# Attention scores issued two steps ahead in some branches, and a later wait at the start of the down products

## The chip, the cores and the metric

The kernel runs on one core of a Trainium2 chip. The time is that of the device in microseconds (us) for one launch of the whole program. Engines are named as in the profile: PE (TensorE matmul), PEld (its weight loads), DVE (VectorE), ACT (ScalarE), POOL (GpSimd), SP (the queue that issues the DMAs).

## The reference

Two layers of a transformer block on 256 latent tokens and 256 context tokens, 1024 wide, all in float32. A layer is a gated feed-forward (up and gate to 2816, down to 1024), a token mixer, and a second feed-forward; each has an RMS norm before and after it, with shift, scale and gate from a conditioning vector. The mixer has four attention branches side by side. Cut to what matters here:

```
A: softmax(q1 k1) - lam * softmax(q2 k2), times v, then a norm      (differential)
B: softmax over a grid window with a bias, plus all context keys   (neighbourhood)
C: grouped queries, q and k normalised per head                    (GQA)
D: band of +-128 tokens plus context keys plus one sink logit       (sliding window)
y = sum_i sigmoid(u @ gate_i) * (branch_i @ w_branch_i);   out = y @ w_out
```

In layer 0 the context tokens pass through the mixer too (512 query columns, T = 512); in layer 1, the last, only the 256 latent tokens are queries (T = 256).

## The kernel before, in words

**Weights.** All weights come in units of 128 x 1024 floats at most (`fetch`, SP), four slots deep. ACT copies a unit to `w_high` in fp32r (L290), DVE writes the rest to `w_low` (L296), both two units ahead of PE (`AHEAD`). One product is then three matmuls for each 128 x 128 block: high x high (L307), low x high (L308), and, in a second pass, high x low (L316). `used` counts finished units.

**The feed-forward.** `Hidden` makes 22 tiles of the hidden vector; DVE finishes a tile with three operations (L693, L697, L699) and then raises `ready`. `Down` reads them: each output row is four units (`DOWN_K` = 6, 5, 6, 5 tiles), so that parts 0 to 2 read tiles 0 to 16 and part 3 reads tiles 17 to 21. Its `tensor` begins with one wait (L787) for all 22 tiles.

**A branch (`Branch`).** The PE program of a branch has two halves. First the *carriers*: the four `mix` units of the branch before (its output times `w_branch`, `mix_unit`, banks 6 and 7 for even c, 4 and 5 for odd c), and then `ahead` gate units of this branch (`window_part`), beside which DVE and ACT prepare q and k (`ropes`, `keep_qk`). Each gate unit is taken out of its bank by ACT (`window_taken`: tanh at L1154, a plain copy at L1156 for the projections of the next branch). On ACT the order for carrier g is: split of a later unit, `window_taken(g)`, then the `keep_qk` items of g. `ahead` is 5, 6 and 2 for B, C and D in layer 1, and 2 for D in layer 0. Gate 0 is taken only when the branch before is wholly merged, since `gate` is reused.

Then the *steps*: J = 16 in layer 0, 8 in layer 1. One step is two heads of 128 queries against 512 (or 256) keys:

- PE `scores(j)` (L1084) into banks 0 and 1, after `expd(j)`, that is when the exponentials of step j-1 have read those banks;
- DVE `row_max(j)`: bias in B (L1380) or mask in D (L1386), the maximum (L1390), and one small operation (L1401), in D three (L1395, L1398, L1399);
- ACT `exps(j)`: two exponentials (L1230) into `prob`, in D a small one before (L1228);
- DVE `scale_probs(j)`: reciprocal and two multiplications (L1422, L1425), in D an addition before (L1409);
- PE `flip(j)`: transposes (L1094) into banks 2 and 3; ACT `keep_probs(j)` (L1240) copies them out;
- every second step PE `mix(p)` (L1107) into bank 4 + p % 2; ACT `high_of_out` (L1253) and DVE `low_of_out` (L1432) read it.

Between them stand the rest of the window units, spread over the steps by a fixed table of weights (`points`), each in two parts, "high" (L307, L308) and "low" (L316), in bank 6 + w % 2. For the later unit w the wait is for `taken(w - 1)`, so that one product can run while the one before it is taken out. Each engine executes its list in order:

```
PE : scores(j+1), part, [mix], flip(j), part
DVE: row_max(j+1), split, scale_probs(j+1), [low_of_out], split
ACT: exps(j+1), part's results, keep_probs(j), [high_of_out], part's results
```

After the last branch `Merge` runs the four mix units of D and `Out` the output product.

Of the kernel before, what the change touches and what calls it, by code (L numbers as in the profile page):

```python
# [158 lines left out]
def build(nc, tokens, small, cond, weights, mods, na_rows, h_kept, c_kept, out, stop=None):  # L159
    STARTS, N_UNITS = unit_starts()  # L160
    WIDTHS = [DOWN_K[u % 4] if name.startswith("down") else 8 for layer in range(DEPTH) for name, count in layer_units(layer) for u in range(count)]
    with ExitStack() as ctx:
# [611 lines left out]
        class Down(Result):  # L774
# [11 lines left out]
            def tensor(self, pe):  # L786
                pe.wait_ge(self.hidden.ready.sem, self.hidden.ready.at(FT))  # L787

                def two_rows(i, last):
                    for e, unit in enumerate(self.units):  # L790
                        n0 = self.n0 + e
                        n = n0 + len(self.units) * i
                        r, part = unit
                        if part == 0 and past(2 * i + r - 1):
                            pe.wait_ge(self.freed.sem, self.freed.at(2 * i + r - 1))
                        k0 = sum(DOWN_K[:part])
                        product(pe, n, n0, [(ps[:, r, 0:self.T], [(w, k0 + w) for w in range(DOWN_K[part])])],
                                lambda k: hid_high[:, k, 0:self.T], lambda k: hid_low[:, k, 0:self.T],
                                first=part == 0, last=part == 3)
                self.rows(two_rows)  # L800
# [70 lines left out]
        class Branch(Stage):  # L871
# [4 lines left out]
            def __init__(self, layer, index, T, norm, before):  # L876
# [3 lines left out]
                self.tiles = BT + 2 * self.nk  # L880

                self.roped, self.normed = b != "B", b == "C"

# [60 lines left out]
                self.sunk = signals.new("sink_shifted", J if b == "D" else 0)  # L944
                self.expd = signals.new("exp_ready", J)
                self.sums = signals.new("sum_steps", 3 * J)
                self.probs = signals.new("probs_ready", J)
# [40 lines left out]
            def values(self, v, tt):  # L988

                return v[:, tt, 0:self.nk * P], ps[:, tt, 0:self.nk * P]  # L990

            def head_items(self, c):

                return [i for i in range(len(self.prep)) if self.normed and i // 2 == c]
# [21 lines left out]
            def window_part(self, pe, w, part):  # L1016
                kind, t, W = self.window[w]
                n = self.n_window + w
                outs = [(ps[:, 6 + w % 2, 0:W], [(k, k) for k in range(KT)])]
                if part == "low":  # L1020
                    product_low(pe, n, n, outs, lambda k: u_high[:, k, 0:W])
                    return
                if w >= 2:
                    pe.wait_ge(self.taken.sem, self.taken.at(w - 1))
                elif self.before:
                    pe.wait_ge(self.before.merged.sem, self.before.merged.at(6))
                else:
                    pe.wait_ge(self.projected.sem, self.projected.at(self.tiles))
                product_high(pe, n, n, outs, lambda k: u_high[:, k, 0:W], lambda k: u_low[:, k, 0:W])
# [5 lines left out]
            def mix_unit(self, pe, c):  # L1035

                if c == 0:
                    pe.wait_ge(self.taken.sem, self.taken.at(len(self.window)))
                if c >= 2:
                    pe.wait_ge(self.merged.sem, self.merged.at(2 * c - 2))  # L1040
                T, n, b0 = self.T, self.n_mix + c, 6 - 2 * (c % 2)
                product(pe, n, n, [(ps[:, b0 + r, 0:T], [(4 * r + k, k) for k in range(BT)]) for r in range(2)],
                        lambda k: q_high[:, k, 0:T], lambda k: q_low[:, k, 0:T])

            def tensor(self, pe):
# [31 lines left out]
                def scores(j):  # L1077
                    t, q, key, nkeys = self.steps[j]
                    kt = t if self.nk == BT else 0
                    if past(j):  # L1080
                        pe.wait_ge(self.expd.sem, self.expd.at(j))
                    for s in range(2):
                        rows = slice(s * HD, (s + 1) * HD)
                        m = pe.matmul(ps[:, s, 0:nkeys], q_all[rows, t, q:q + P], k_all[rows, kt, key:key + nkeys], start=True, stop=True)  # L1084
                    m.then_inc(self.scored.sem, 1)
# [11 lines left out]
                def mix(p):  # L1097
                    t, _, key, nkeys = self.steps[2 * p]
                    vt = t if self.nk == BT else 0
                    pe.wait_ge(self.pt_made.sem, self.pt_made.at(2 * p + 2))  # L1100
                    if p >= 2:
                        pe.wait_ge(self.o_done.sem, self.o_done.at(p - 1))
                    n, ns = nkeys // P, 1 if b == "A" else 2
                    for c in range(n):
                        for s in range(ns):
                            rows = slice(s * P // ns, (s + 1) * P // ns)
                            m = pe.matmul(ps[rows, 4 + p % 2, 0:S_X], v_all[:, key // P + c, vt * P:(vt + 1) * P][:, rows], pt[:, p % 2, s, c],  # L1107
                                          start=c == 0, stop=c == n - 1)
                    m.then_inc(self.mixed.sem, 1)
# [7 lines left out]

                scores(0)
                self.window_parts(pe, 0)
                for j in range(J):  # L1120
                    if j + 1 < J:
                        scores(j + 1)
                    self.window_parts(pe, 1 + 2 * j)
                    if b == "A" and j % 2 and j >= 3:
                        sub_sum((j - 3) // 2)
                    if j % 2 == 0 and j:
                        mix(j // 2 - 1)
                    flip(j)
                    self.window_parts(pe, 2 + 2 * j)
# [19 lines left out]
            def window_taken(self, act, w):  # L1149
# [3 lines left out]
                if kind == "gate":  # L1153
                    i = act.activation(gate[:, t, 0:W], ps[:, 6 + w % 2, 0:W], ACT.Tanh, scale=0.5)  # L1154
                else:
                    i = act.activation(proj[:, t, 0:W], ps[:, 6 + w % 2, 0:W], ACT.Copy)  # L1156
                i.then_inc(self.taken.sem, 1)
# [29 lines left out]
            def scalar(self, act):  # L1187
# [33 lines left out]
                def exps(j):  # L1221
# [7 lines left out]
                    for s in range(2):  # L1229
                        e = act.activation(prob[:, j % 2, s, 0:nkeys], ps[:, s, 0:nkeys], ACT.Exp,  # L1230
                                           bias=stat[:, j % 2, 1, s:s + 1], scale=SCALE, accum_out=stat[:, j % 2, 2, s:s + 1])
# [11 lines left out]
                def high_of_out(p):  # L1243
# [3 lines left out]
                    if b == "A":  # L1247
# [4 lines left out]
                        return  # L1252
                    act.activation(q_high[:, t, q:q + S_X], ps[:, bank, 0:S_X], ACT.Copy).then_inc(self.o_high.sem, 1)  # L1253

# [76 lines left out]
            def merge(self, dve, c):  # L1331

                b0, T = 6 - 2 * (c % 2), self.T
                dve.wait_ge(used.sem, self.n_mix + c + 1)
# [14 lines left out]
            def vector(self, dve):  # L1349
# [22 lines left out]
                def row_max(j):  # L1372
                    t, q, key, nkeys = self.steps[j]
                    f = sum(step[2] == 0 for step in self.steps[:j])
                    both = ps[:, 0:2]
                    dve.wait_ge(self.scored.sem, self.scored.at(j + 1))
# [15 lines left out]
                    if b == "D":  # L1392
                        sink = smv("sink", self.l, DEPTH, "p (t s) -> p t s", s=2)[:, t]

                        dve.scalar_tensor_tensor(out=stat[:, j % 2, 5], in0=stat[:, j % 2, 0], scalar=SCALE, in1=sink,  # L1395
                                                 op0=ALU.mult, op1=ALU.max).then_inc(self.sums.sem, 1)
                        dve.wait_ge(self.sums.sem, self.sums.at(3 * j + 1))
                        dve.tensor_tensor(stat[:, j % 2, 3], sink, stat[:, j % 2, 5], ALU.subtract).then_inc(self.sunk.sem, 1)  # L1398
# [4 lines left out]
                def scale_probs(j):  # L1403
# [4 lines left out]
                    if b == "D":  # L1408
                        dve.tensor_tensor(st[:, 5], st[:, 2], st[:, 4], ALU.add).then_inc(self.sums.sem, 1)  # L1409
                        dve.wait_ge(self.sums.sem, self.sums.at(3 * j + 2))  # L1410
# [17 lines left out]
                def low_of_out(p):  # L1428
                    t, q, _, _ = self.steps[2 * p]
                    bank = 4 + p % 2  # L1430
                    dve.wait_ge(self.o_high.sem, self.o_high.at(p + 1))
                    dve.tensor_tensor(q_low[:, t, q:q + S_X], ps[:, bank, 0:S_X], q_high[:, t, q:q + S_X], ALU.subtract)\  # L1432
                        .then_inc(self.o_low.sem, 1)
# [12 lines left out]

                row_max(0)
                self.window_splits(dve, split_low, 0)
                scale_probs(0)
                for j in range(J):  # L1450
                    if j + 1 < J:
                        row_max(j + 1)
                    self.window_splits(dve, split_low, 1 + 2 * j)
# [114 lines left out]
        for layer in range(DEPTH):  # L1568
            last = layer == DEPTH - 1
            for j in range(3):  # L1570
# [3 lines left out]
                if j == 1:  # L1574
                    T = S_X if last else S_ALL
                    branches = []
                    for i in range(len(BRANCHES)):
                        branches.append(Branch(layer, i, T, norm, branches[-1] if branches else None))
                        mixers[layer, BRANCHES[i]] = branches[-1]
                    stages += branches  # L1580
                    merge = Merge(layer, T, branches[-1])
# [221 lines left out]
```

## Time and profile before

| | |
|---|---|
| median of 3 runs | 2626.4 us (2624.17 to 2632.94) |
| the profiled execution | 2630.91 us, of which span 2629.1 us |
| PE busy | 2458.7 us (94%) |
| DVE busy | 1584.3 us (60%) |
| ACT busy | 1068.2 us (41%) |
| mean granted clock of PE | 0.975 |

The span is from the first to the last instruction. A granted clock of 1.00 is 2.4 GHz, 0.50 is 1.2 GHz; a stretch between them had both. "Idle before" an instruction is time in which its engine ran nothing, and the name behind it is what released it.

### The profile page before, as it was taken

The page shows a single profiled execution, that of the slowest core. Times are in us where ns is not written, and L with a number is a line of the kernel's source. Part 1 is how long each engine was busy: PE and PEld are TensorE (multiplying, and loading weights), DVE is VectorE, ACT ScalarE, POOL GpSimd, SP SyncE. Part 2 cuts the span into 40 slices and gives each one's busy share as a digit, 9 for nine tenths or more (in the row PEclk, how much of TensorE's full clock was granted, in tenths as well). Part 3 has the DMA queues.
Part 4 walks back from the last instruction along what each step waited for, and adds up shares of the span by engine and source line. Part 5 has one row for each costly group of instructions (what it writes and reads, how often), then busy time and mean ns, then how long its engine had stood idle before and what let it go on. Part 6 is the DMA issues. An engine that isn't in the chain of part 4 may idle for free.

```text
span 2629.1 us, 31723 instructions
## 1 busy us (share of the span) xinstructions
PE 2458.7 (94%) x12584; PEld 1987.2 (76%) x12584; DVE 1584.3 (60%) x2620; ACT 1068.2 (41%) x1842; POOL 27.3 (1%) x43
## 2 busy tenths in 40 slices
PE   6999998999999998889999989999989999978998
PEld 3788786877767675667887868887868777767998
DVE  2888777345455455689886873333455456567654
ACT  4222234355354534452222352222345555545444
POOL 0000000000000000000000000000000000000000
PEclk8999999999999999999999999999999999989999
DMA  5655454221212121126555522222333243223554
GB/s 225 224 192 192 165 189 141 90 72 65 99 62 72 56 81 64 60 93 216 192 192 170 185 93 96 97 96 84 101 113 128 74 147 109 89 97 112 178 171 157
DMA packets 98069, 331.42 MB, mean 126 GB/s; under 512 B 11009, under 2 KB 12033, under 8 KB 97281
## 3 DMA queue, kind: packets, MB, share of 16 engines
q1 hardware_dynamic: 97922, 329.39, 36.3%
q8 instruction: 100, 1.64, 0.2%
q14 instruction: 47, 0.39, 0.0%
HBM read 323.06 MB, written 6.29 MB: 125 GB/s over the span
## 4 chain that ended last, share of the span: by engine, by line
PE 78%; DVE 10%; ACT 7%; issue 3%; DMA 2%; SPq 0%; POOL 0%; DVEq 0%; ACTq 0%
PE ps L307 23%; PE ps L316 23%; PE ps L308 23%; PE ps L1107 2%; PE ps L1084 2%; DVE stat L1390 2%; ACT prob L1230 2%; PE ps L1094 2%; PE ps L620 2%; ACT w_high L290 1%; DVE w_low L296 1%; DMA raw<-in_weights 1%; DVE tmp L602 1%; ACT pt L1240 1%; ACT sq L551 1%
## 5 line engine op out<-in xcount | busy, mean ns | idle before, releaser
L296 DVE TENSOR_TENSOR w_low<-raw,w_high 128x1024 fp32r<-128x1024 f32 (+1 forms) x488 | 552.4, 1135 | 598.2 <-ACT w_high L290 597.6
L307 PE MATMUL ps<-u_high,w_high 128*128 128x512 f32 (+1 forms) x2304 | 816.6, 365 | 13.1 <-DVE hid_low L699 11.1
L290 ACT ACTIVATE w_high<-raw 128x1024 fp32r<-128x1024 f32 (+1 forms) x488 | 482.0, 990 | 816.5 <-DMA raw<-in_weights 815.9
L308 PE MATMUL ps<-u_low,w_high 128*128 128x512 f32 (+1 forms) x2304 | 807.6, 361 | 0.0
L316 PE MATMUL ps<-u_high,w_low 128*128 128x512 f32 (+1 forms) x2496 | 545.0, 362 | 4.8 <-DVE w_low L296 4.8
L307 PEld LDWEIGHTS ps<-u_high,w_high 128*128 128x128 f32 x2304 | 444.3, 193 | 104.0 <-issue 22.1
L316 PEld LDWEIGHTS ps<-u_high,w_low 128*128 128x128 f32 x2496 | 422.8, 190 | 93.2 <-issue 20.1
L308 PEld LDWEIGHTS ps<-u_low,w_high 128*128 128x128 f32 x2304 | 444.4, 193 | 62.2
L379 DVE CUSTOM_DVE_ANT_0 ps<-mod_raw,c_all,smalls 128x1024 f32<-128x1024 f32 x256 | 319.0, 1287 | 1.1 <-DMA mod_raw<-in_mods 1.0
L307 PE MATMUL ps<-hid_high,w_high 128*128 128x512 f32 (+1 forms) x704 | 252.3, 367 | 9.0 <-DVE hid_low L699 9.0
L308 PE MATMUL ps<-hid_low,w_high 128*128 128x512 f32 (+1 forms) x704 | 251.9, 367 | 0.0
L1230 ACT ACTIVATE prob<-ps,stat 128x512 f32<-128x512 f32 (+1 forms) x192 | 116.3, 610 | 161.8 <-DVE stat L1401 161.8
L316 PE MATMUL ps<-hid_high,w_low 128*128 128x512 f32 (+1 forms) x704 | 161.6, 363 | 0.0
L307 PEld LDWEIGHTS ps<-hid_high,w_high 128*128 128x128 f32 x704 | 134.6, 191 | 31.6 <-DVE hid_low L699 10.4
L308 PEld LDWEIGHTS ps<-hid_low,w_high 128*128 128x128 f32 x704 | 134.6, 191 | 21.1
L1084 PE MATMUL ps<-k_all,q_all 64*128 64x512 f32 (+1 forms) x384 | 96.2, 578 | 45.1 <-ACT prob L1230 33.3
L316 PEld LDWEIGHTS ps<-hid_high,w_low 128*128 128x128 f32 x704 | 122.5, 189 | 20.7
L1390 DVE TENSOR_REDUCE stat<-ps 128x2 f32<-128x1024 f32 (+1 forms) x96 | 100.2, 1044 | 38.8 <-PE ps L1084 37.4
L693 DVE TENSOR_TENSOR hid<-silu_g,ps 128x512 f32<-128x512 f32 (+1 forms) x88 | 54.2, 616 | 91.8 <-PE ps L316 91.4
L1240 ACT ACTIVATE pt<-ps 128x1024 f32<-128x1024 f32 (+2 forms) x96 | 76.3, 795 | 73.7 <-PE ps L1094 73.5
L620 PE MATMUL ps<-u_high,w_high 128*128 128x512 f32 (+1 forms) x192 | 56.8, 423 | 37.6 <-ACT u_high L555 37.6
L1094 PE MATMUL ps<-smalls,prob 128*128 128x128 f32 x560 | 80.5, 279 | 10.5 <-DVE prob L1425 9.1
(147 smaller groups left out, 2160.1 us busy)
## 6 DMA issues: line engine op xcount, KB each, us to landing
raw<-in_weights SPq DMA_DIRECT2D x360, 512.0 KB, 3.5
mod_raw<-in_mods SPq DMA_DIRECT2D x128, 512.0 KB, 4.5
raw<-in_weights SPq DMA_DIRECT2D x64, 384.0 KB, 3.0
raw<-in_weights SPq DMA_DIRECT2D x64, 320.0 KB, 2.8
mod_first<-in_mods SPq DMA_DIRECT2D x16, 512.0 KB, 13.4
h_kept<-h SPq DMA_DIRECT2D x16, 256.0 KB, 2.0
na_bias<-in_na_rows SPq DMA_DIRECT2D x16, 256.0 KB, 4.0
h<-h_kept SPq DMA_DIRECT2D x2, 2048.0 KB, 8.2
```

Source lines behind the costliest of these rows:

```text
L290: act.activation(w_high[:, s, 0:width], raw[s][:, 0:width], ACT.Copy).then_inc(high_made.sem, 1)
L296: dve.tensor_tensor(w_low[s][:, 0:width], raw[s][:, 0:width], w_high[:, s, 0:width], ALU.subtract).then_inc(low_made.sem, 1)
L307: pe.matmul(o, w_high[:, s, w], x_high(x), start=first and a == 0, stop=False)
L308: pe.matmul(o, w_high[:, s, w], x_low(x), start=False, stop=False)
L316: done = pe.matmul(o, w_low[s][:, w], x_high(x), start=False, stop=last and a == len(terms) - 1)
L379: done = dve.tensor_tensor_reduce(out=ps[:, 4 + 2 * s:6 + 2 * s].rearrange("p a b -> p (a b)"), in0=mod_raw[i % MOD_SLOTS][:, :], in1=c_al ...
L620: pe.matmul(ps[:, banks[e], 0:W], w_high[:, (self.n0 + e) % SLOTS, k], x[:, k, 0:W], start=k == 0 and x is u_high, stop=False)
L1084: m = pe.matmul(ps[:, s, 0:nkeys], q_all[rows, t, q:q + P], k_all[rows, kt, key:key + nkeys], start=True, stop=True)
L1094: m = pe.transpose(ps[:, 2 + s, c * P:(c + 1) * P], prob[:, j % 2, s, c * P:(c + 1) * P], ident)
L1230: e = act.activation(prob[:, j % 2, s, 0:nkeys], ps[:, s, 0:nkeys], ACT.Exp, bias=stat[:, j % 2, 1, s:s + 1], scale=SCALE, accum_out=stat[ ...
L1240: act.activation(pt[:, j // 2 % 2, 0:ns, 0:nkeys // P, half], ps[:, 2:2 + ns, 0:nkeys].rearrange("p s (c q) -> p s c q", q=P), ACT.Copy).t ...
L1390: dve.tensor_reduce(stat[:, j % 2, 0], both[:, :, 0:nkeys], AX.X, ALU.max).then_inc(self.maxed.sem, 1)
```

## The change

In D of both layers and in B and C of layer 1 (`deep`) the scores go two steps ahead, in banks 0 and 1 for even steps and 6 and 7 for odd steps. For that the window units have one bank (5) in place of two, `mix` has one bank (4) in place of two, and the mix units of the branch before change places (even c in 4 and 5, odd c in 6 and 7). DVE's row maxima go two steps ahead as well. In D the semaphore `sum_steps` is split in two, as the order of its increments changes. In `Down` the wait for all 22 hidden tiles becomes a wait for 21 tiles ahead of parts 0 to 2 of the first row, and for 22 ahead of its part 3.

```diff
             def tensor(self, pe):            # Down
-                pe.wait_ge(self.hidden.ready.sem, self.hidden.ready.at(FT))
...
+                        if i == 0 and r == 0:
+                            pe.wait_ge(self.hidden.ready.sem, self.hidden.ready.at(FT if part == 3 else FT - 1))
...
+                self.deep = b == "D" or b in "BC" and T == S_X
+                self.early = 2 if self.deep else 1
...
+            def score_bank(self, j):
+                return 6 * (j % 2) if self.deep else 0
+            def window_bank(self, w):
+                return 5 if self.deep else 6 + w % 2
+            def out_of(self, p):
+                return ps[:, 4 if self.deep else 4 + p % 2, 0:S_X]
+            def mix_bank(self, c):
+                return 4 + 2 * (c % 2) if self.mix_swapped else 6 - 2 * (c % 2)
...
             def window_part(self, pe, w, part):
-                if w >= 2:
-                    pe.wait_ge(self.taken.sem, self.taken.at(w - 1))
+                banks = 1 if self.deep else 2
+                if w >= banks:
+                    pe.wait_ge(self.taken.sem, self.taken.at(w - banks + 1))
...
             def scores(j):
-                    if past(j):
-                        pe.wait_ge(self.expd.sem, self.expd.at(j))
+                    if past(j + 1 - self.early):
+                        pe.wait_ge(self.expd.sem, self.expd.at(j + 1 - self.early))
...
             def mix(p):
-                    if p >= 2:
-                        pe.wait_ge(self.o_done.sem, self.o_done.at(p - 1))
+                    if p >= (1 if self.deep else 2):
+                        pe.wait_ge(self.o_done.sem, self.o_done.at(p if self.deep else p - 1))
...
-                scores(0)
+                for j in range(self.early):
+                    scores(j)
                 self.window_parts(pe, 0)
                 for j in range(J):
-                    if j + 1 < J:
-                        scores(j + 1)
+                    if j + self.early < J:
+                        scores(j + self.early)
...
-                row_max(0)
+                for j in range(self.early):
+                    row_max(j)
                 self.window_splits(dve, split_low, 0)
                 scale_probs(0)
                 for j in range(J):
-                    if j + 1 < J:
-                        row_max(j + 1)
+                    if j + self.early < J:
+                        row_max(j + self.early)
...
+                    for i, branch in enumerate(branches):
+                        branch.mix_swapped = i + 1 < len(branches) and branches[i + 1].deep
```

The lists of the other engines keep their order, so that ACT still does `exps(j+1)` ahead of `keep_probs(j)`. Which parts of the window stand between the steps stays as it was.

## Rows read from the trace of the kernel before

**Rows 1.** The page: busy times, and the down products' first matmuls with their waits.
```profile
PE 2458.7 (94%) x12584; PEld 1987.2 (76%) x12584; DVE 1584.3 (60%) x2620; ACT 1068.2 (41%) x1842; POOL 27.3 (1%) x43
...
L307 PE MATMUL ps<-hid_high,w_high 128*128 128x512 f32 (+1 forms) x704 | 252.3, 367 | 9.0 <-DVE hid_low L699 9.0
```

**Rows 2.** Windows over the steps of D (layer 0), then B, C, D (layer 1).
```profile
core 0: us, PE busy (x) PEld busy (x) DVE busy (x) ACT busy (x) POOL busy (x), PEclk, DMA share, GB/s
...
984.00:1081.00 97.00, 78.33 (x401) 50.77 (x402) 51.33 (x150) 44.79 (x118) 0.00 (x0) 0.95 0.15 54
...
2125.00:2190.00 65.00, 57.75 (x376) 44.28 (x376) 37.19 (x62) 32.02 (x64) 0.00 (x0) 0.97 0.26 90
...
2228.00:2287.00 59.00, 54.38 (x356) 40.38 (x357) 29.84 (x52) 30.74 (x60) 0.00 (x0) 1.00 0.21 73
...
2308.60:2368.60 60.00, 48.37 (x304) 35.73 (x304) 35.91 (x84) 28.55 (x65) 0.00 (x0) 0.89 0.23 86
```

**Rows 3.** Waits, 984 to 1081 us, D of layer 0: total us, times, longest.
```profile
PE ps L1084 <- ACT prob L1230: 10.5, 7, 3.2
...
PE ps L1094 <- DVE prob L1425: 4.4, 4, 2.3
```

**Rows 4.** Waits, 2125 to 2190 us, B of layer 1.
```profile
PE ps L1084 <- ACT prob L1230: 4.2, 5, 0.9
...
PE ps L1094 <- DVE prob L1425: 2.1, 1, 2.1
```

**Rows 5.** Waits, 2228 to 2287 us, C of layer 1.
```profile
PE ps L1084 <- ACT prob L1230: 3.0, 3, 1.0
```

**Rows 6.** Waits, 2308.6 to 2368.6 us, D of layer 1.
```profile
PE ps L1084 <- ACT prob L1230: 8.2, 4, 3.5
...
PE ps L1094 <- DVE prob L1425: 1.8, 2, 1.3
```

**Rows 7.** Window after the first down start, L307 alone: us, PE, PEld, PEclk, DMA.
```profile
297.70:302.00 4.30, 3.32 (x6) 1.69 (x6) 0.60 0.28 107
```

**Rows 8.** Timeline of DVE in D, layer 0: start, us, operation, [idle before].
```profile
985.40 0.43 DVE L1386 TENSOR_TENSOR ps<-ps,smalls 128x256 f32<-128x256 f32 x1 [4.40 <-PE ps L1084]
985.87 1.23 DVE L1390 TENSOR_REDUCE stat<-ps 128x2 f32<-128x1024 f32 x1
...
991.65 0.88 DVE L1425 TENSOR_SCALAR prob<-prob,stat 128x512 f32<-128x512 f32 x2
```

**Rows 9.** Timeline of PE around three hand-overs of a bank, same columns.
```profile
984.22 1.13 PE L1084 MATMUL ps<-k_all,q_all 64*128 64x512 f32 x4 [1.72 <-ACT q_all L1185]
...
2118.02 1.12 PE L316 MATMUL ps<-u_high,w_low 128*128 128x256 f32 x8
...
2362.82 1.10 PE L1094 MATMUL ps<-smalls,prob 128*128 128x128 f32 x8 [1.32 <-DVE prob L1425]
2365.03 1.95 PE L1107 MATMUL ps<-pt,v_all 128*64 128x256 f32 x16 [1.11 <-ACT pt L1240]
```

**Rows 10.** Timeline of ACT in the carriers of D, B, C, D.
```profile
982.54 0.60 ACT L1154 ACTIVATE gate<-ps 128x512 f32<-128x512 f32 x1 [2.79 <-PE ps L316]
...
2113.46 1.28 ACT L1154 ACT_TABLE_LOAD   x1 [0.89 <-PE ps L316]
2114.76 0.39 ACT L1154 ACTIVATE gate<-ps 128x256 f32<-128x256 f32 x1
...
2119.18 0.38 ACT L1154 ACTIVATE gate<-ps 128x256 f32<-128x256 f32 x1 [1.13 <-PE ps L316]
...
2218.11 0.36 ACT L1154 ACTIVATE gate<-ps 128x256 f32<-128x256 f32 x1
...
2305.36 0.39 ACT L1154 ACTIVATE gate<-ps 128x256 f32<-128x256 f32 x1 [4.87 <-DVE acc L1347]
...
2307.85 0.75 ACT L1185 ACTIVATE q_all<-proj 128x256 f32<-128x256 f32 x2 [0.27 <-DVE proj L1322]
```

**Rows 11.** Window over B's later steps, with four waits of 0.8 to 0.9 us.
```profile
2138.00:2174.00 36.00, 32.35 (x237) 24.63 (x237) 22.79 (x40) 19.75 (x40) 0.00 (x0) 1.00 0.33 110
```

More of the change, by code:

```diff
@@ L945, in __init__ @@
                 self.expd = signals.new("exp_ready", J)
+                self.capped = signals.new("row_max_with_sink", J if b == "D" else 0)
                 self.sums = signals.new("sum_steps", 3 * J)
@@ L1018, in window_part @@
                 n = self.n_window + w
-                outs = [(ps[:, 6 + w % 2, 0:W], [(k, k) for k in range(KT)])]
+                outs = [(ps[:, self.window_bank(w), 0:W], [(k, k) for k in range(KT)])]
                 if part == "low":
@@ L1040, in mix_unit @@
                     pe.wait_ge(self.merged.sem, self.merged.at(2 * c - 2))
-                T, n, b0 = self.T, self.n_mix + c, 6 - 2 * (c % 2)
+                T, n, b0 = self.T, self.n_mix + c, self.mix_bank(c)
                 product(pe, n, n, [(ps[:, b0 + r, 0:T], [(4 * r + k, k) for k in range(BT)]) for r in range(2)],
@@ L1079, in scores @@
                     kt = t if self.nk == BT else 0
-                    if past(j):
-                        pe.wait_ge(self.expd.sem, self.expd.at(j))
+                    if past(j + 1 - self.early):
+                        pe.wait_ge(self.expd.sem, self.expd.at(j + 1 - self.early))
                     for s in range(2):
                         rows = slice(s * HD, (s + 1) * HD)
-                        m = pe.matmul(ps[:, s, 0:nkeys], q_all[rows, t, q:q + P], k_all[rows, kt, key:key + nkeys], start=True, stop=True)
+                        m = pe.matmul(ps[:, self.score_bank(j) + s, 0:nkeys], q_all[rows, t, q:q + P], k_all[rows, kt, key:key + nkeys], start=True, stop=True)
                     m.then_inc(self.scored.sem, 1)
@@ L1106, in mix @@
                             rows = slice(s * P // ns, (s + 1) * P // ns)
-                            m = pe.matmul(ps[rows, 4 + p % 2, 0:S_X], v_all[:, key // P + c, vt * P:(vt + 1) * P][:, rows], pt[:, p % 2, s, c],
+                            m = pe.matmul(self.out_of(p)[rows], v_all[:, key // P + c, vt * P:(vt + 1) * P][:, rows], pt[:, p % 2, s, c],
                                           start=c == 0, stop=c == n - 1)
@@ L1153, in window_taken @@
                 if kind == "gate":
-                    i = act.activation(gate[:, t, 0:W], ps[:, 6 + w % 2, 0:W], ACT.Tanh, scale=0.5)
+                    i = act.activation(gate[:, t, 0:W], ps[:, self.window_bank(w), 0:W], ACT.Tanh, scale=0.5)
                 else:
-                    i = act.activation(proj[:, t, 0:W], ps[:, 6 + w % 2, 0:W], ACT.Copy)
+                    i = act.activation(proj[:, t, 0:W], ps[:, self.window_bank(w), 0:W], ACT.Copy)
                 i.then_inc(self.taken.sem, 1)
@@ L1229, in exps @@
                     for s in range(2):
-                        e = act.activation(prob[:, j % 2, s, 0:nkeys], ps[:, s, 0:nkeys], ACT.Exp,
+                        e = act.activation(prob[:, j % 2, s, 0:nkeys], ps[:, self.score_bank(j) + s, 0:nkeys], ACT.Exp,
                                            bias=stat[:, j % 2, 1, s:s + 1], scale=SCALE, accum_out=stat[:, j % 2, 2, s:s + 1])
@@ L1252, in high_of_out @@
                         return
-                    act.activation(q_high[:, t, q:q + S_X], ps[:, bank, 0:S_X], ACT.Copy).then_inc(self.o_high.sem, 1)
+                    act.activation(q_high[:, t, q:q + S_X], self.out_of(p), ACT.Copy).then_inc(self.o_high.sem, 1)
                 def sub_root(p):
@@ L1331, in merge @@
             def merge(self, dve, c):
-                b0, T = 6 - 2 * (c % 2), self.T
+                b0, T = self.mix_bank(c), self.T
                 dve.wait_ge(used.sem, self.n_mix + c + 1)
@@ L1374, in row_max @@
                     f = sum(step[2] == 0 for step in self.steps[:j])
-                    both = ps[:, 0:2]
+                    both = ps[:, self.score_bank(j):self.score_bank(j) + 2]
                     dve.wait_ge(self.scored.sem, self.scored.at(j + 1))
@@ L1395, in row_max @@
                         dve.scalar_tensor_tensor(out=stat[:, j % 2, 5], in0=stat[:, j % 2, 0], scalar=SCALE, in1=sink,
-                                                 op0=ALU.mult, op1=ALU.max).then_inc(self.sums.sem, 1)
-                        dve.wait_ge(self.sums.sem, self.sums.at(3 * j + 1))
+                                                 op0=ALU.mult, op1=ALU.max).then_inc(self.capped.sem, 1)
+                        dve.wait_ge(self.capped.sem, self.capped.at(j + 1))
                         dve.tensor_tensor(stat[:, j % 2, 3], sink, stat[:, j % 2, 5], ALU.subtract).then_inc(self.sunk.sem, 1)
@@ L1408, in scale_probs @@
                     if b == "D":
-                        dve.tensor_tensor(st[:, 5], st[:, 2], st[:, 4], ALU.add).then_inc(self.sums.sem, 1)
+                        dve.tensor_tensor(st[:, 5], st[:, 2], st[:, 4], ALU.add).then_inc(self.sums.sem, 2)
                         dve.wait_ge(self.sums.sem, self.sums.at(3 * j + 2))
@@ L1429, in low_of_out @@
                     t, q, _, _ = self.steps[2 * p]
-                    bank = 4 + p % 2
                     dve.wait_ge(self.o_high.sem, self.o_high.at(p + 1))
-                    dve.tensor_tensor(q_low[:, t, q:q + S_X], ps[:, bank, 0:S_X], q_high[:, t, q:q + S_X], ALU.subtract)\
+                    dve.tensor_tensor(q_low[:, t, q:q + S_X], self.out_of(p), q_high[:, t, q:q + S_X], ALU.subtract)\
                         .then_inc(self.o_low.sem, 1)
```

## The prediction

> **What bounds the kernel now.** I read the page first: PE is busy 94% of the span, DVE 60%, ACT 41% [rows 1]. So time is to be had only where PE sits idle, or where its clock is low. The view of windows by stage says where that is [rows 2]: over the steps of D in layer 0 PE is busy 78.3 of 97 us at a mean granted clock of 0.95, over those of D in layer 1 48.4 of 60 us at 0.89; B and C of layer 1 are fuller (57.8 of 65, 54.4 of 59). In none of the four is DVE or ACT busy for more than 60% of the stretch, so there PE waits for latency and not for a full engine. The waits name it: `scores` (L1084) waits for the exponentials of the step before, 10.5, 4.2, 3.0 and 8.2 us [rows 3 to 6], 25.9 us in all. This is a ring: scores, row maximum, exponentials, scores again, since all steps share banks 0 and 1. The rest are flips that wait for DVE's probabilities, 4.4, 2.1, 0.9 and 1.8 us (0.9 in C, in the same view), and waits of flips and mixes for ACT's copies at the end of a branch, such as the 1.11 us in [rows 9]. The reader should see in [rows 8] that the ring is long although no piece of it is: mask 0.43, maximum 1.23, three small operations, 2.2 us on DVE, and then some 1.5 us on ACT.
>
> **Down products.** The first matmul of the four down products waits 9.0 us in all for `hid_low` [rows 1], since DVE's three operations on the last hidden tile stand between the last product and the first. The change asks for 21 tiles there, and tile 21 (counted from 1) is ready two units earlier. Part 3, which needs the 22nd, comes 17 blocks x 3 matmuls later, over 6 us even at 0.12 us each. No wait takes its place: the first two units' splits stand ahead of the tile's operations in DVE's list, and the third's low half is wanted two units later. Gain 9.0 us. There is a second part: after the stall the granted clock is 0.60 over 4.30 us [rows 7], and the same is seen behind two more of the four (not behind the last one, of 1.30 us). PE has no pause there, so each loses 0.40 x 4.3 = 1.7 us. If the stall goes, so should the slow stretch, with PE busy up to that point: 3 x 1.7 = 5.1 us. Gain of this part 14.1 us; between 9.0 (the slow stretches stay) and 14.1.
>
> **Scores two ahead, where it helps.** Now `scores(j+2)` needs `exps(j)`, and a whole step's work of PE lies between. What is late next?
>
> *Steady steps.* DVE must do `row_max(j+2)` before `scale_probs(j+1)`, which `flip(j+1)` waits for. In D that is 2.2 + 1.2 us and 0.3 of signals after `scores(j+2)`, plus 1.1 where a split stands between. PE has in that time `flip(j)` 0.85, `scores(j+3)` 1.06, every second step a mix of 1.9 us or half of that, and in most steps a part of a window unit (3.6 or 1.8 us in layer 0, 1.9 or 1.0 in layer 1). The sums are 3.7 to 4.8 against 4 to 7 us: no wait, but only just on steps without a window part. `exps` stands behind `window_taken` in ACT's list, so after a "low" part it ends 0.25 + 0.5 + 1.0 to 1.5 us later, against 1.5 to 2.5 us of PE work: two waits of 0.4 and 0.8 us in D of layer 0, none in layer 1.
>
> *First steps.* `row_max(1)` now stands ahead of `scale_probs(0)`, so that the first flip comes no earlier than before; PE has the scores of step 2 done by then. Left at this point: 1.7 us in D of layer 0, 1.9 in B, 1.2 in C, 0.8 + 1.3 in D of layer 1.
>
> *Last steps.* Flip 15 (or 7) waits for the copy of the one before, the last mix for its copy: 1.5 us in D of layer 0 and 1.0 in D of layer 1 stay.
>
> So, gaps before minus gaps left: D layer 0, 17.7 (10.5, 4.4 and 2.8 behind ACT's copies) - 1.7 - 1.2 - 1.5 = 13.3. B, 6.3 - 1.9 = 4.4. C, 3.9 - 1.2 = 2.7. D layer 1, 8.2 + 1.8 + 1.1 = 11.1, minus 0.8, 1.3, 1.0 and 0.6 for the hand-over named below = 7.4. The clock: D of layer 0 has 0.05 x 97 = 4.9 us less of it, some of that in idle time; I take 4.0. D of layer 1 has 0.11 x 60 = 6.6, of which 5.3 fell on matmuls; a stall of 1.3 us at its start is left, so I take 4.5. B's one slow stretch stays, as its first stall stays. If half the slow stretches stay, 4 us less.
>
> **What one window bank costs.** Now each window unit starts only when ACT has taken the one before. The trace has no such hand-over in these branches, since two banks alternate: units follow each other without a pause. From below it is 0, where scores or a flip stand between; from above I take the row of the same chain plus what it delays. ACT starts 0.03 to 0.04 us after PE's last matmul (2118.02 + 1.12, then 2119.18 [rows 9, 10]), takes 0.38 us for 256 columns and 0.60 for 512, and PE starts 0.05 us later. PE would have issued its next matmul 0.16 us before the last one ends. That is 0.6 us for 256 columns and 0.85 for 512.
>
> Within the steps only two pairs of units touch, one in C and one in D of layer 1, as their scores between are gone: 0.6 us each. Elsewhere a flip (0.85 us) or more stands between. In the carriers all gates touch:
> - D layer 0, one hand-over, 0.85 us. It moves `keep_qk` behind it, which `scores(0)` waits for [rows 9], so nothing hides it.
> - B, four. The first has the table load on ACT ahead of the tanh: 1.28 us, the tanh from 2114.76 to 2115.15 against a product that ended at 2113.4 [rows 10], so 2.0 us; then 3 x 0.63. In all 3.9.
> - C, five. The first is as in B, but there DVE's rope already makes PE wait later on, for 2.5 us at 2218.8. ACT takes gate 2 at 2218.11 [rows 10], behind `k_all`, and gate 3 now starts only then. Followed through, `scores(0)` is 1.1 us later, or 2.5 with a slow stretch moved; I take 1.5.
> - D layer 1, one. Gate 0 is taken at 2305.36, held by the merge [rows 10]. So gate 1 starts at 2305.8, 1.9 us later than now, and ends at 2308.75; ACT then has 0.38 and 0.75 us to do before `scores(0)`: 2309.95 for 2308.65, that is 1.3 us.
>
> The one mix bank costs nothing: `o_low` of the mix before is made a step and a half earlier, on an engine with time left. `Merge`'s mixes, SP's queue and the h reload keep their order; weights come at 53 to 90 GB/s in these stretches [rows 2] and are not late.
>
> **A rule on ACT's table.** The row shows 1.28 us for the load and the tanh 1.30 us behind its start. The Trainium skill (ScalarE: Activation LUTs, What ACT_TABLE_LOAD costs) gives 1283 ns and a drain of some 1380 ns more for every switch. By it the first hand-over in B and in C would cost 1.4 us more each, 2.8 us in the sum; the trace does not bear that out.
>
> **The sum.** Down 14.1; D layer 0 13.3 + 4.0 - 0.85 = 16.5; B 4.4 - 3.9 = 0.5; C 2.7 - 0.6 - 1.5 = 0.6; D layer 1 7.4 + 4.5 - 1.3 = 10.6. Together 42.3 us. The profiled execution took 2630.91 us, 4.5 over the median of the runs shown, and would take 2588.6. Against the median: 2626.4 - 42.3 = 2584.1, and I put down 2585.
>
> **Rivals.**
> 1. *The wait only moves.* DVE's list, now with a row maximum between exponentials and probabilities, is late at every flip on steps without a window part, and the 25.9 us come back as L1094 waiting for L1425. For it: the steady sums above are within 1 us of each other. Against it: DVE is busy for 60% at most. Then the down part stays, and a third of the rest: 14.1 + 9 = 23, and 2603. Chance 0.17.
> 2. *Single banks decide; slower.* In ACT's list `exps(j+1)` stands ahead of `window_taken`. If ACT has not begun it when a "low" part ends, PE waits for 1.5 us of exponentials and the 0.6 of the hand-over. At all 29 window units of the steps that is 61 us, against 42 of gain: 2626.4 + 19 = 2645. It decides from some 20 units on. Against it: ACT is busy at most 52% there (30.7 of 59 us [rows 2]), and `exps(j+1)` has its row maximum a step early. Chance 0.04.
> 3. *The clock falls in the carriers.* Ten hand-overs of 0.6 us or more follow each other in B and C. In this trace four waits of 0.8 to 0.9 us within 36 us left the clock at 1.00 [rows 11], so I don't expect it. If it fell in half of the 38 us of the two carriers' gates and of D's, at 1.7 us for each 4.3, that is 8 us, and the slow stretches in the steps might stay too, 8 more: 2601. Chance 0.14. The Trainium skill (TensorE: Matmul & The Clock Gate, A second HAM failure mode: psum-queue depth-cycling) tells of a kernel in which many short idles between groups made the clock fall and rise again; by that rule this rival would be the outcome.
> 4. *More than forecast.* First-step stalls shrink too and every slow stretch goes: 10 us more, 2575. Chance 0.10.
>
> **How the numbers follow.** The forecast has 0.55; its own range is 2574 to 2597. With rivals 1, 3 and 4 inside, 8 in 10 lie in 2569 to 2607. A measurement of this kernel can tell about 0.3% (8 us) from no change. Only rival 2 is slower, and a mild form of it, or of 1 and 3 together, gives no change: faster 0.92, same 0.05, slower 0.03.
>
> **What would show it.** Right: no L307 waiting for L699 at the down products and a clock of 1.00 behind them; L1084 waiting for L1230 down from 25.9 to below 3 us; new waits of L307 for L1154 of 0.6 to 0.85 us each, 2.0 at the first of B and C; the steps of D in some 80 and 50 us. Wrong: L1094 waiting for L1425 above 10 us (rival 1), L307 waiting for L1154 above 20 us (rival 2), or clocks below 1.00 in B's and C's gates (rival 3).

## The result and the profile after

The changed kernel takes 2587.31 us (median of 4; 2580.96 to 2588.93) against 2629.67 us of the kernel before on the same chip: ratio 0.9835, 95% interval 0.9808 to 0.9863, some 43 us faster. In its profiled execution the span is 2587.1 us.

PE is busy for 2451.2 us of it, DVE for 1584.3 and ACT for 1068.5. From the page of the changed kernel, groups of PE (busy us, mean ns | idle before and its releasers); L1103 is now `scores`, L1113 the flips, L1126 `mix`, L1174 the tanh of the gates:

```profile
L307 PE MATMUL ps<-hid_high,w_high 128*128 128x512 f32 (+1 forms) x704 | 249.0, 362 | 0.0
...
L1103 PE MATMUL ps<-k_all,q_all 64*128 64x512 f32 (+1 forms) x384 | 94.5, 573 | 19.9 <-ACT q_all L1205 11.1
...
L1113 PE MATMUL ps<-smalls,prob 128*128 128x128 f32 x560 | 79.7, 277 | 7.2 <-DVE prob L1445 5.9
```

The 9.0 us ahead of the down products [rows 1] are 0.0. The idle time ahead of the scores fell from 45.1 to 19.9 us over the whole kernel, and what is left of it is mostly q and k, which come as late as before. The same stages as in [rows 2], with the same columns, in windows set to their new ends:

```profile
982.30:1062.00 79.70, 74.10 (x401) 48.63 (x402) 51.09 (x150) 44.46 (x118) 0.00 (x0) 0.98 0.18 66
2101.70:2161.80 60.10, 57.16 (x376) 44.23 (x376) 36.85 (x61) 32.75 (x63) 0.00 (x0) 0.97 0.29 97
2201.20:2257.10 55.90, 53.74 (x353) 40.11 (x353) 29.94 (x52) 31.02 (x60) 0.00 (x0) 1.00 0.23 76
2280.40:2327.60 47.20, 42.76 (x305) 31.42 (x305) 34.16 (x83) 28.79 (x66) 0.00 (x0) 1.00 0.31 112
2083.00:2102.00 19.00, 15.00 (x107) 13.88 (x105) 6.65 (x7) 8.53 (x15) 0.00 (x0) 0.91 0.38 133
```

The first four answer to [rows 2]: the same work in 80, 60, 56 and 47 us. DVE and ACT do in them what they did before. The fifth is B's gates, with PE idle for 4 of 19 us.

The waits of PE (total us, times, longest) over D of layer 0 and over D of layer 1 answer to [rows 3] and [rows 6]:

```profile
PE ps L1113 <- DVE prob L1445: 1.9, 1, 1.9
...
PE ps L1113 <- ACT pt L1260: 1.4, 2, 0.8
...
PE ps L1126 <- ACT pt L1260: 0.7, 1, 0.7
PE ps L1103 <- ACT prob L1250: 0.5, 1, 0.5
```
```profile
PE ps L1113 <- DVE prob L1445: 1.1, 1, 1.1
PE ps L1126 <- ACT pt L1260: 1.1, 1, 1.1
...
PE ps L1103 <- ACT prob L1250: 0.9, 1, 0.9
PE ps L307 <- ACT gate L1174: 0.7, 1, 0.7
```

In the four branches the 25.9 us of scores waiting for exponentials are 1.4 us. The price stands in the gates of B, in the timeline of PE (start, us, idle before):

```profile
2086.07 0.39 PE L307 MATMUL ps<-u_high,w_high 128*128 128x256 f32 x1 [1.81 <-ACT gate L1174]
2090.86 0.43 PE L307 MATMUL ps<-u_high,w_high 128*128 128x256 f32 x1 [0.47 <-ACT gate L1174]
```

Each is a hand-over of the one bank, the first with ACT's table load in it; two more of 0.47 us follow. The units start 4.8 us apart once and then 3.6, where two banks gave 2.9 (2113.22 to 2116.10 us in the kernel before).

The kernels can be laid side by side by stage. These are us between the same PE instructions of the profiled executions ("gates" is from the first mix unit of the branch before to the first scores; D0 is layer 0, where it starts at the turning of v; the others are layer 1):

```
                      D0           B            C            D        four down
                   gates steps  gates steps  gates steps  gates steps   starts
before              35.1  96.6   26.9  65.2   37.1  59.0   21.6  60.0   stall
changed             36.1  79.3   32.4  60.2   39.0  56.3   23.0  47.1   none
e1 down alone       35.1  93.5   26.9  65.3   37.0  59.0   21.6  59.8   none
e2 scores alone     36.1  79.3   32.6  60.2   39.3  56.3   23.0  47.1   stall
e3 D alone          36.1  79.3   26.9  65.3   37.1  59.0   23.0  47.1   none
e4 banks 5 and 4    35.1  77.7   26.9  58.7   37.0  56.3   21.6  47.6   none
e5 max one ahead    36.1  93.0   32.4  71.7   39.3  61.7   23.0  60.7   none
e6 one window bank  36.1  95.4   32.6  75.5   38.7  63.2   24.5  63.3   stall
e7 first max late   36.1  79.3   32.5  60.2   39.2  58.5   23.0  51.2   none
e8 B and C too      35.1  79.3   26.9  60.3   35.7  56.3   21.6  47.6   none
e9 late split       36.1  88.7   32.7  70.8   39.3  60.0   24.5  58.7   none
e10 best            35.1  76.0   26.9  57.1   35.7  55.1   21.6  46.2   none
e11 taken first     36.1  87.8   31.2  64.5   38.7  57.9   23.0  61.5   none
e12 e9 and e11      36.1  88.6   31.2  63.6   38.7  57.0   24.5  58.4   none
```

Compare the rows before and e1 first: their branches are the same, and seven of the eight stages agree within 0.2 us. The steps of D0 do not, 96.6 against 93.5 us. The kernel before had its clock at 0.95 there and e1 at 0.98. So 3 us of that one entry belong to the execution and not to the kernel.

### The profile page after: what moved, and what is told of

Read it like the earlier page. It is cut to its first block, busy times and chain, and to the rows that moved or that the text cites. A ratio compares the mean times of both kernels' runs of the same rounds, so it can differ in the third digit from the quotient of the medians.

```text
span 2587.1 us, 31763 instructions
## 1 busy us (share of the span) xinstructions
PE 2451.2 (95%) x12584; PEld 1981.8 (77%) x12584; DVE 1584.3 (61%) x2620; ACT 1068.5 (41%) x1842; POOL 27.3 (1%) x43
## 4 chain that ended last, share of the span: by engine, by line
PE 86%; DVE 6%; ACT 5%; issue 2%; DMA 1%; SPq 0%; POOL 0%; DVEq 0%; ACTq 0%
PE ps L316 25%; PE ps L307 25%; PE ps L308 24%; PE ps L1126 3%; PE ps L1103 3%; PE ps L1113 2%; PE ps L620 2%; DVE tmp L602 1%; ACT w_high L290 1%; ACT prob L1250 1%; DVE h L571 1%; ACT sq L551 1%; DMA raw<-in_weights 1%; DVE stat L1410 1%; DVE w_low L296 1%
## 5 line engine op out<-in xcount | busy, mean ns | idle before, releaser
L307 PE MATMUL ps<-u_high,w_high 128*128 128x512 f32 (+1 forms) x2304 | 812.1, 364 | 23.6 <-DVE hid_low L699 11.0
L307 PEld LDWEIGHTS ps<-u_high,w_high 128*128 128x128 f32 x2304 | 439.5, 191 | 116.1 <-issue 19.0
L307 PE MATMUL ps<-hid_high,w_high 128*128 128x512 f32 (+1 forms) x704 | 249.0, 362 | 0.0
L307 PEld LDWEIGHTS ps<-hid_high,w_high 128*128 128x128 f32 x704 | 132.9, 189 | 20.6
L1103 PE MATMUL ps<-k_all,q_all 64*128 64x512 f32 (+1 forms) x384 | 94.5, 573 | 19.9 <-ACT q_all L1205 11.1
L1113 PE MATMUL ps<-smalls,prob 128*128 128x128 f32 x560 | 79.7, 277 | 7.2 <-DVE prob L1445 5.9
## 6 DMA issues: line engine op xcount, KB each, us to landing
mod_first<-in_mods SPq DMA_DIRECT2D x16, 512.0 KB, 12.9
```

What stands on the lines that cost most here:

```text
L307: pe.matmul(o, w_high[:, s, w], x_high(x), start=first and a == 0, stop=False)
L1103: m = pe.matmul(ps[:, self.score_bank(j) + s, 0:nkeys], q_all[rows, t, q:q + P], k_all[rows, kt, key:key + nkeys], start=True, stop=True)
L1113: m = pe.transpose(ps[:, 2 + s, c * P:(c + 1) * P], prob[:, j % 2, s, c * P:(c + 1) * P], ident)
```

## The experiments

Each time is given with the ratio to the kernel before and its 95% interval.

**e1, the down part alone.** The edit is the `Down` part of the diff.

> The kernel before with the down products' later wait alone. Theory (the stall and the slow stretch behind it both go): 9.0 us of waits and 3 x 1.7 us of slow clock, 14 us faster than before, ratio 0.9946, granted clock 1.00 behind all four starts. Rival (the slow stretches come by where the stage falls in time, not by the stall): 9 us faster, ratio 0.9966, and slow stretches near the starts remain.

Measured: 2612.42 us, 0.9939 (0.9927 to 0.9951), 16.0 us faster, with an interval of 13 to 19. The theory holds: 9 us is outside. The windows of this kernel after the first three starts, for L307, answer to [rows 7] (the fourth had no slow stretch before and has none here):

```profile
294.70:299.00 4.30, 2.51 (x7) 1.13 (x7) 1.00 0.78 266
1398.20:1402.50 4.30, 2.54 (x7) 1.13 (x6) 1.00 0.79 249
1777.10:1781.40 4.30, 2.55 (x7) 1.16 (x7) 1.00 0.25 80
```

The granted clock is 1.00, 2.4 GHz, where it was 0.60 [rows 7].

**e2, the scores alone.** The changed kernel with the old wait in `Down`.

> The changed kernel with the old wait at the down products. Theory (the parts add): 28 us faster than before, ratio 0.9893; the four stalls of 9.0 us and three slow stretches are back. Rival (the down part had a share in the branches too, by the phase of the clock): more or less than 28 by over 5 us.

Measured: 2600.77 us, 0.9892 (0.9879 to 0.9905), 28.4 us. 16.0 and 28.4 make 44.4, and the whole gave 43: the parts add, within the intervals. In its trace the four starts wait 9.3 us in all again, and the clock behind the first three is 0.60, 0.60 and 0.66.

**e3, D alone two ahead.**

```diff
-self.deep = b == "D" or b in "BC" and T == S_X
+self.deep = b == "D"
```

> The changed kernel with the scores two ahead in D alone (B and C of layer 1 as before, with two window banks). Theory (in B and C the gain in the steps is eaten by the hand-overs of the one window bank in the gates: 5.0 against 5.4 in B, 2.5 against 1.9 in C): no difference from the changed kernel within 2 us, 42 us faster than before. Rival (B and C carry their share of the 25.9 us of waits, the hand-overs are hidden): 7 us slower than the changed kernel.

Measured: 2589.76 us, 0.9849 (0.9836 to 0.9862), 39.7 us. The medians are 2.4 us apart, those of the profiled spans 1.2, and the intervals overlap; the 7 us of the rival are not there. So B and C brought next to nothing. The table shows why: B won 5.0 us in its steps and lost 5.5 in its gates, C won 2.7 and lost 1.9. B's steps repeat well: 65.2 to 65.3 us in the kernel before, e1 and e3, and 60.2 in the changed kernel, e2 and e7 (58.7 in e4, whose steps are the same).

**e4, two banks for the gates.** Bank 4 is idle until the first mix of the branch.

```diff
 def window_bank(self, w):
+    if self.deep and w < self.ahead:
+        return 5 - (self.ahead - w) % 2
     return 5 if self.deep else 6 + w % 2
...
-    banks = 1 if self.deep else 2
+    banks = 1 if self.deep and w > self.ahead else 2
```

> The changed kernel, but the gate units ahead of the steps alternate between banks 5 and 4 (4 is idle until the first mix), so that only units within the steps share one bank. Theory (each hand-over in the gates is on the path): D layer 0 1.0, B 5.4, C 1.9, D layer 1 1.3, together 9.6 us faster than the changed kernel, 52 us faster than before. Rival (PE waits for q and k ahead of the first scores anyway, so the time comes back there): under 3 us faster than the changed kernel.

Measured: 2577.17 us, 0.9801 (0.9789 to 0.9814), 52.3 us faster than before. That is some 9 to 10 us faster than the changed kernel, as the theory had it. The gates take what they took before the change (35.1, 26.9, 37.0, 21.6). All hand-overs of the gates were on the path.

**e5, row maxima one step ahead.** PE and its banks stay as changed, DVE's list is as before.

```diff
-for j in range(self.early):
-    row_max(j)
+row_max(0)
...
-    if j + self.early < J:
-        row_max(j + self.early)
+    if j + 1 < J:
+        row_max(j + 1)
```

> The changed kernel, but DVE takes the row maxima one step ahead as before, while PE issues the scores two ahead. Theory (the two pairs of banks alone break the ring; row maximum, exponentials and probabilities in turn take 2.2 + 1.7 + 1.2 = 5.1 us a step against 5.3 to 6 us of PE): within 4 us of the changed kernel, with the first flip of each branch earlier. Rival (DVE's order is as needed as the banks; without it the wait moves to the flips): 10 us or more slower than the changed kernel, L1113 or its like waiting for L1445 over 10 us more.

Measured: 2633.45 us, 1.0012 (1.0003 to 1.0021). My theory fell: 46 us are lost against the changed kernel, the whole gain of the scores and more. This kernel still has the later wait in `Down`, so the fair measure of the banks alone is e1, 0.9939: against that, two pairs of banks with DVE's old order cost some 19 us. The rival has the size right, but not the place. Flips wait for DVE 4.5 us more (10.4 for 5.9), scores for exponentials 11.5 more (20.2 for 8.7), and most of all window units for ACT's taking, as the group of this kernel shows:

```profile
L307 PE MATMUL ps<-u_high,w_high 128*128 128x512 f32 (+1 forms) x2304 | 819.4, 366 | 37.8 <-ACT gate L1174 18.4 <-DVE hid_low L699 11.1 <-ACT proj L1176 6.9
```

These are 25.3 us for 11.3, of which 9.4 are the gates'. The three together are 30 us; the rest is in PE's busy time, 2465.5 for 2451.2 us, at a mean clock of 0.974 for 0.983. Why the scores wait is seen at ACT, whose exponentials of D wait for DVE's row maximum. First the changed kernel, then this one (the kernel before had 61.4):

```profile
ACT stat L1248 <- DVE stat L1419: 7.6, 3, 3.4
```
```profile
ACT stat L1248 <- DVE stat L1419: 56.6, 23, 4.5
```

Its DVE timeline over one step in D of layer 1 shows what I had left out of the ring:

```profile
2325.15 0.42 DVE L1406 TENSOR_TENSOR ps<-ps,smalls 128x256 f32<-128x256 f32 x1
...
2329.86 1.23 DVE L296 TENSOR_TENSOR w_low<-raw,w_high 128x1024 fp32r<-128x1024 f32 x1 [2.56 <-ACT w_high L290]
...
2331.39 0.88 DVE L1445 TENSOR_SCALAR prob<-prob,stat 128x512 f32<-128x512 f32 x2
2332.19 0.42 DVE L1406 TENSOR_TENSOR ps<-ps,smalls 128x256 f32<-128x256 f32 x1
```

From one row maximum to the next are 7.0 us, not 5.1: DVE's split waits 2.56 us for ACT's, which stands behind the exponentials, and the scaling stands behind the split.

**e6, one window bank in the old order.** The kernel before, with `window_bank` 6 for all units of the four branches and a wait for `taken(w)`.

> The kernel before with one window bank in place of two in D and in layer 1's B and C, and nothing else. Theory: the gates cost what they cost in the changed kernel, 1.0 + 5.4 + 1.9 + 1.3 = 9.6 us, and in the steps there is more, since in the old order ACT's exponentials of the next step stand ahead of the taking and come 3.9 us after the scores: some 2 us at each of five units in B and C, 15 us slower than before in all. Rival (within the steps something always stands between two units): 10 us slower or less.

Measured: 2659.92 us, 1.0110 (1.0092 to 1.0127), 29 us slower, twice what I expected. The gates cost 1.0, 5.7, 1.6 and 2.9 us, against 1.0, 5.4, 1.9 and 1.3; the steps of B cost 10.3 us more, C 4.2, D of layer 1 3.3, and those of D of layer 0 nothing. This is the mechanism of rival 2 of the prediction, and it is real where the exponentials come late. 28 us of L307 wait for the taking here, 11 in the changed kernel.

**e7, the first row maximum of step 1 late.**

```diff
-for j in range(self.early):
-    row_max(j)
+row_max(0)
 self.window_splits(dve, split_low, 0)
 scale_probs(0)
+for j in range(1, self.early):
+    row_max(j)
```

> The changed kernel, but the row maximum of step 1 stands behind the probabilities of step 0 in DVE's list. Theory (the first flip comes 1 to 2 us earlier and the second as much later): within 2 us of the changed kernel. Rival (the first flips' waits, 1.9, 2.0, 0.9 and 1.1 us, are lost time): 4 to 6 us faster.

Measured: 2596.07 us, 0.9871 (0.9854 to 0.9889), 9 us slower than the changed kernel by the medians. Neither: D of layer 1 loses 4.1 us and C 2.2. The flips still wait 5.9 us for DVE in all. What is new is that in D of layer 1 the scores wait 3.4 us for exponentials, for 0.9 before, and the clock is 0.97 for 1.00; in C one gate unit waits 2.0 us for its bank.

**e9, e11 and e12, on top of e5.** Two candidates for what e5 lost: DVE's split in the ring (R), and ACT's taking behind the exponentials (H).

```diff
 # e9, DVE                                   # e11, ACT
-self.window_splits(dve, ..., 1 + 2 * j)    +self.window_results(act, 1 + 2 * j)
 scale_probs(j + 1)                          exps(j + 1)
+self.window_splits(dve, ..., 1 + 2 * j)    -self.window_results(act, 1 + 2 * j)
```

> The kernel with the maxima one step ahead (e5_max_one_ahead), but in the deep branches DVE's low split stands behind scale_probs and not ahead of it. Theory R (that kernel is paced by a ring on DVE and ACT: row maximum 2.0, exponentials 1.6, high split 1.05, low split 1.15, scaling 1.2 = 7.0 us a step that has a split; behind the scaling the split leaves the wait for ACT's high split out of the ring): about 1.5 us less on each of some 29 steps with a split where PE is not the bound, 15 to 30 us faster than e5_max_one_ahead. Theory H (the hand-over of the one window bank, behind the exponentials in ACT's list, is what costs): no more than 5 us faster.

> The kernel with the maxima one step ahead (e5_max_one_ahead), but in the deep branches ACT takes the window unit and splits the next ahead of the exponentials. Theory H: the 25 us of waits of L307 for ACT's taking fall to the 8 us of the gates, 10 to 17 us faster. Theory R: the waits move, since the exponentials now wait for PE's low part; within 5 us of e5_max_one_ahead or slower.

> The maxima one step ahead with both edits: DVE's low split behind the scaling, and ACT's taking ahead of the exponentials. The first alone gave 8 us, the second 16. Theory (they are separate waits, and what is left is DVE's order itself): they add, 24 us faster than e5_max_one_ahead and still some 22 slower than the changed kernel. Rival (they are two ends of one wait, so that either fixes it): no more than 17 us faster than e5_max_one_ahead. Third outcome (the order of the maxima matters only through these two): within 5 us of the changed kernel.

Measured: e9 2625.47 us, 0.9983 (0.9973 to 0.9992), 8 us better than e5, between the two theories (15 to 30, or at most 5); e11 2615.62, 0.9950 (0.9934 to 0.9966), 16 to 18 better, the upper end of H, though the waits for the taking fell only from 25.3 to 14.9 us and not to 8; e12 2618.18, 0.9955 (0.9938 to 0.9971), the same as e11, 15 better than e5, as its rival had it. So they do not add: the taking is the greater part, and the split, once that is done, brings nothing more over all. 31 us of the 46 are left in e12. Scores still wait 23.8 us for exponentials in e11 and 28.9 in e12, for 8.7 in the changed kernel. That the rest is the place of the row maxima itself is the likely reading; but e11 and e12 differ from the changed kernel in these edits too, and it was not taken apart further. What e5 does show is that the place of the maxima, as the only difference, is worth the whole 46 us.

**e8 and e10, better versions.** e8 is e4 with B and C of layer 0 two ahead as well (`self.deep = b != "A"`). e10 is e8 with DVE's split behind the scaling, as in e9, also at the first step.

> The kernel with banks 5 and 4 for the gates (e4_carrier_banks), and the scores two ahead in layer 0's B and C as well. In these the scores wait 3.6 and 1.4 us before. Theory: some 4 us faster than e4_carrier_banks, less 0.9 us for each pair of window units without scores between. Rival (512-column units keep PE full there, one bank only costs): no gain or some us slower.

> The kernel with the scores two ahead in B, C, D of both layers and gates in banks 5 and 4 (e8_deep_in_BCD), with DVE's low split behind scale_probs. With the exponentials a step early DVE's split is waited for by nobody in the steady steps; at the first step the scaling, and so the first flip (5.9 us of waits in all), comes 1 to 2 us earlier. Theory: 3 to 6 us faster than e8_deep_in_BCD. Rival (the low split is then late for PE's low part): slower, with L316 waiting for L296.

Measured: e8 2572.01 us, 0.9777 (0.9760 to 0.9793); e10 2565.06 us, 0.9756 (0.9739 to 0.9773), 64 us faster than before and 21 to 22 faster than the changed kernel. e8 is 5 to 6 us faster than e4, with some 4 forecast: the steps of B in layer 0 take 102.3 us for 106.6. e10 is 5 to 7 us faster than e8, with 3 to 6 forecast, but their intervals overlap. In e10 the flips hardly wait any more, 0.5 us for DVE where the changed kernel and e8 have 5.9.

## Why the prediction was right

The time forecast was 2585, measured 2587.3; the gain forecast 42.3, measured 43. The path, the waits and most of the costs were right. Two things were not: why the ring opens, and the cost of B's gates. And the exact agreement of the total is in part luck, as the single entries below differ by up to 3 us and cancel. By step:

- **Down products**, 14.1 forecast, 16.0 measured alone (13 to 19). Shown by e1: both the stalls and the slow stretches behind them went.
- **Steps of D**, layer 0: 17.3 forecast (13.3 and 4.0 of clock), 17.3 in the stage table; but 3 us of it are slow clock of that one execution before. Against e1 it is 14.2, of which 13.1 are idle time, as forecast, and 1.1 clock where I had 4.0. Layer 1: 11.9 forecast (7.4 and 4.5), 12.9. The waits left are those I named: first flip 1.9 for 1.7, the last ones 1.4 + 0.7 for 1.5, in layer 1 0.9, 1.1, 0.7 and 1.1 for 0.8, 1.3, 0.6 and 1.0. Of the two waits behind a low part in layer 0, 1.2 us forecast, one of 0.5 shows. D of layer 1 lost all its slow clock [rows 2], not a part.
- **Steps of B and C**, 4.4 and 2.1 forecast (the hand-over inside C counted), 5.0 and 2.7.
- **Gates.** D 0.85 and 1.3, in fact 1.0 and 1.4; C 1.5, in fact 1.9; B 3.9, in fact 5.5. The term for B was mis-sized: the four waits with their overlap are 3.9, but the first, 1.81 us, was followed by a slow stretch (clock 0.91 over the 19 us), 1.6 us more, which I had kept out with "I don't expect it". In e11 and e12 the same hand-overs had no slow stretch behind them, and B's gates took 31.2 us, 4.3 more than before: close to the 3.9. Rival 3 (which counts ten hand-overs in B and C; they are nine) came in part: behind the one long hand-over of B and of C the clock fell, behind the short ones it did not.
- **The rule on table switches**, for which the prediction names the Trainium skill (ScalarE: Activation LUTs, What ACT_TABLE_LOAD costs), did not show: in B's gates of the changed kernel the load began at 2084.34 us and the tanh at 2085.63, 1.29 us later, and PE's wait of 1.81 has no room for 1.4 more.
- **Why the ring opens** was right in its result and half wrong in its reason. The prediction puts the ring down to the shared banks 0 and 1 ("since all steps share banks 0 and 1"). e5 has the second pair of banks and is 19 us slower than e1. The prediction weighs DVE's new order almost only as a cost (in the steady steps, the first steps and rival 1) and names its use once, in rival 2. It is what makes the change work: the exponentials' wait for row maxima in D is 7.6 us with it and 56.6 without. The scores then find their bank free, and, by the order of ACT's list, ACT is free sooner to take the window units, so that the one bank costs little in the steps. Without it the one bank costs up to 10 us in a branch (B in e6; in e5 B's steps are 11.5 us longer than in the changed kernel).
- Rival 1 (the wait moves to the flips) did not come: 5.9 us of flips waiting for DVE, for 9.1 before.

That B and C brought nothing (e3) was in the numbers, 0.5 and 0.6, but the text didn't draw the conclusion.

## What to carry to other kernels

When a ring of engines over shared banks is to be opened, move the consumer's list as far ahead as the producer's: more banks alone cost 19 us here, where more banks and the moved list together gained 28. Before giving up a double buffer for it, look for the stages in which another bank is idle; here that was 10 us. Count a stall of some 2 us on PE with the slow matmuls that can follow it: at the down products they were worth half as much again as the stall.

## What the runs showed of the hardware

A slow stretch, with the granted clock at 0.50 (1.2 GHz), followed several stalls of PE of 1.8 us and more: 1.81 in B's gates of the changed kernel, and 1.97, 2.82 and 2.87 at the down starts of the kernel before. None followed the 1.30 us at the fourth start, nor a row of waits of 0.47. But the length of the stall does not decide it. PE waits 2.24 us ahead of the first scores of C in layer 0 in both kernels, and the clock over the 6 us behind it is 1.00 in the kernel before and 0.72 in the changed one. The first flip of D in layer 0 waits 2.26 us in the one and 1.89 in the other, and it is the longer wait that kept the clock at 1.00 (0.72 behind the other). Nor did it fall behind 1.78 us in D's gates of layer 1. The same stall of 1.81 us in B's gates, first in the changed kernel, then in e11:

```profile
2086.10:2092.10 6.00, 5.53 (x34) 5.23 (x35) 1.24 (x2) 2.49 (x4) 0.00 (x0) 0.72 0.20 72
```
```profile
2091.70:2097.70 6.00, 5.53 (x44) 5.32 (x45) 2.39 (x2) 2.53 (x4) 0.00 (x0) 1.00 0.36 132
```

In the same 6 us PE ran 34 matmuls in the one and 44 in the other. What decides between the two is not shown by these runs. The same work in stages that no edit touched also had slow stretches in one kernel and not in another: from the third down start to the end of layer 1's A the executions without the stall took 302.8 to 303.0 or 305.8 to 305.9 us. A difference of 3 us between two kernels in one profile is therefore no evidence by itself, and the ratios above rest on the timed rounds.
